# Causal mask of the prompt attention: an addition on VectorE in place of a mask product on TensorE

## What is computed

```python
def fox_attend(q, k, v, cq, ck, q_pos, k_pos):
    s = jnp.einsum('bqhd,bkhd->bhqk', q, k) * (1.0 / math.sqrt(HEAD_DIM))
    decay = jnp.transpose(cq, (0, 2, 1))[..., :, None] - jnp.transpose(ck, (0, 2, 1))[..., None, :]
    mask = k_pos[None, :] <= q_pos[:, None]
    s = jnp.where(mask[None, None], s + decay, -jnp.inf)
    p = jax.nn.softmax(s, axis=-1)
    return jnp.einsum('bhqk,bkhd->bqhd', p.astype(v.dtype), v)
```

## Time and profile before

| what | value |
|---|---|
| median of three runs | 2351.63 us |
| the profiled execution | 2349.69 us |
| its span, first to last instruction | 2347.9 us |
| mean granted TensorE clock | 0.994 |
| PE busy over the span | 2284.9 us (97%) |
| DVE, ACT, POOL busy | 1033.8, 581.4, 632.4 us |

### The profile page before, as it was taken

One profiled execution on the slowest core, in us unless ns is written; L12 is line 12 of the kernel. 1 busy time (PEld: TensorE's weight loads), 2 busy tenths in 40 slices (PEclk: granted clock), 3 DMA queues, 4 the chain that ended last, 5 costly groups with the idle time before them and its releaser, 6 DMA issues. The chain is left out here.

```text
span 2347.9 us, 36305 instructions
## 1 busy us (share of the span) xinstructions
PE 2284.9 (97%) x14220; PEld 2093.6 (89%) x14220; DVE 1033.8 (44%) x1728; ACT 581.4 (25%) x1270; POOL 632.4 (27%) x444
## 2 busy tenths in 40 slices
PE   7999999999999999999989999999999999999998
PEld 7999999999999967777756666799999999999997
DVE  6743332433433756442146777434433323333331
ACT  6420110110100433332135666322110100101101
POOL 6622222232332512100000110453222323222221
PEclk9999999999999999999999999999999999999999
DMA  4111111111111214444464554111111111111111
GB/s 140 40 46 54 46 46 46 46 46 46 46 46 46 90 54 150 134 147 143 155 182 96 126 114 100 36 46 46 45 46 46 46 46 46 46 46 51 48 46 75
DMA packets 194328, 169.96 MB, mean 72 GB/s; under 512 B 28608, under 2 KB 168944, under 8 KB 194167
## 3 DMA queue, kind: packets, MB, share of 16 engines
q1 hardware_dynamic: 153225, 137.71, 20.4%
q10 hardware_dynamic: 40950, 30.02, 4.0%
HBM read 137.55 MB, written 30.50 MB: 72 GB/s over the span
## 5 line engine op out<-in xcount | busy, mean ns | idle before, releaser
L341 PE MATMUL ps<-xn_hi,w_lo 128*128 128x352 f32 x1536 | 497.1, 324 | 5.0 <-DVE h L564 3.2
L494 PE MATMUL ps<-hid_hi,w_lo 128*128 128x352 f32 x1536 | 495.4, 323 | 0.0
L494 PE MATMUL ps<-hid_lo,w_hi 128*128 128x352 f32 x1536 | 492.7, 321 | 0.0
L341 PE MATMUL ps<-xn_lo,w_hi 128*128 128x352 f32 x1536 | 492.4, 321 | 0.0
L341 PE MATMUL ps<-xn_hi,w_hi 128*128 128x352 f32 x1536 | 492.3, 320 | 0.0
L494 PE MATMUL ps<-hid_hi,w_hi 128*128 128x352 f32 x1536 | 492.2, 320 | 0.0
L318 POOL CAST w_hi<-w_raw 128x1024 fp32r<-128x1024 f32 x136 | 142.8, 1050 | 1008.0 <-issue 529.0
L564 DVE TENSOR_TENSOR h<-ps,h 128x352 f32<-128x352 f32 x384 | 198.5, 522 | 446.3 <-PE ps L494 446.3
L532 ACT ACTIVATE tmp_b<-tmp_a 128x352 f32<-128x352 f32 x192 | 95.1, 499 | 1090.6 <-DVE tmp_a L550 1090.6
L320 POOL TENSOR_TENSOR w_lo<-w_raw,w_hi 128x1024 fp32r<-128x1024 f32 x136 | 328.4, 2415 | 10.9
L341 PEld LDWEIGHTS ps<-xn_hi,w_lo 128*128 128x128 f32 x1536 | 288.1, 188 | 7.3 <-DVE h L564 4.3
(11 more groups left out here) (228 smaller groups left out, 2577.4 us busy)
## 6 DMA issues: line engine op xcount, KB each, us to landing
w_raw<-in_w_up SPq DMA_DIRECT2D x64, 512.0 KB, 4.0
w_raw<-in_w_down SPq DMA_DIRECT2D x64, 512.0 KB, 3.4
out<-tok_out ACTq DMA_DIRECT2D x32, 256.0 KB, 2.1
qk_dram<-turn_hi ACTq DMA_DIRECT2D x32, 256.0 KB, 2.4
qk_dram<-turn_lo ACTq DMA_DIRECT2D x32, 256.0 KB, 2.9
k_page<-in_cache_k SPq DMA_DIRECT2D x32, 256.0 KB, 3.3
v_page<-in_cache_v SPq DMA_DIRECT2D x16, 512.0 KB, 9.2
q_a<-qk_dram SPq DMA_DIRECT2D x32, 256.0 KB
```

Of the source, the lines that this page charges most:

```text
L341: last = pe.matmul(ps[:, bank, 0:CH], w, x(k, c), start=(k == 0 and i == 0), stop=(k == nk - 1 and i == 2))
L494: last = pe.matmul(ps[:, NC * (dm % 2) + c, 0:CH], w, x, start=(k == 0 and i == 0), stop=(k == GT - 1 and i == 2))
```

## The change

The mask product leaves score(n); the last product of q_b and k_b now increments q_full. In top(n) DVE first adds an fp32 triangle from SBUF to the diagonal piece in PSUM, in place, waits for that with a semaphore of its own, q_cut, and then takes the maximum over the whole block as before. ident_b and causal_b, both bf16, go from SBUF, and an fp32 tile named causal comes. POOL makes it with a memset and the same selection; its cast of the identity goes. PE no longer waits for the constants, and DVE waits for both steps at block 0.

```diff
@@ prompt_pe, score(n)
-                    pe.matmul(ps[:, b + s // 512, 0:c], q_b[e][0:HD + 2, i * P:w], k_b[e][0:HD + 2, s:s + c],
-                              start=False, stop=(s + c < w))
-                at_ = i * P % 512
-                pe.matmul(ps[:, b + i * P // 512, at_:at_ + P], ident_b[:, :], causal_b[:, :], start=False,
-                          stop=True).then_inc(q_full, 1)
+                    last = pe.matmul(ps[:, b + s // 512, 0:c], q_b[e][0:HD + 2, i * P:w], k_b[e][0:HD + 2, s:s + c],
+                              start=False, stop=True)
+                last.then_inc(q_full, 1)
@@ prompt_dve, top(n)
                 dve.wait_ge(q_full, n + 1)
+                if n == 0:
+                    dve.wait_ge(a_const, 2)
+                diag = scores_of(i)[:, i * P:(i + 1) * P]
+                dve.tensor_tensor(diag, diag, causal[:, :], ALU.add).then_inc(q_cut, 1)
+                dve.wait_ge(q_cut, n + 1)
                 dve.tensor_reduce(stat[:, 0, n % 4:n % 4 + 1], scores_of(i), AX, ALU.max, negate=True).then_inc(q_max, 1)
@@ prompt_const
-            pool.tensor_copy(ident_b[:, :], ident[:, :]).then_inc(a_const, 1)
-            pool.memset(causal_b[:, :], 0.0).then_inc(a_const, 1)
-            pool.wait_ge(a_const, 2)
-            pool.affine_select(out=causal_b[:, :], in_=causal_b[:, :], compare_op=ALU.is_ge, fill=-BIG, base=0,
+            pool.memset(causal[:, :], 0.0).then_inc(a_const, 1)
+            pool.wait_ge(a_const, 1)
+            pool.affine_select(out=causal[:, :], in_=causal[:, :], compare_op=ALU.is_ge, fill=-BIG, base=0,
@@ the stream of PE
-            pe.wait_ge(a_const, 3)
             prompt_pe(pe)
```

More of the change, by code:

```diff
@@ L208, in decoder_step @@
         v_h = [at(f"v_h{i}", [P, NQ, HD], F32, o_tok_at + i * NQ * HD * 4) for i in range(2)]
-        ident_b = att("ident_b", [P, P], BF16)
-        causal_b = att("causal_b", [P, P], BF16)
+        causal = att("causal", [P, P])
         stat = att("stat", [P, 3, 4])
@@ L954, in pe @@
                 pe.drain().then_inc(w_used, 1)
-        o_cut = sem("o_cut")
+        o_cut, q_cut = sem("o_cut"), sem("q_cut")
         proj_o = ProjO()
```

## The result

The changed kernel takes 2372.38 us (median of six runs, 2369.54 to 2375.93) where the kernel before takes 2351.43 (six runs, 2350.84 to 2353.38): a ratio of 1.0088, 95% interval 1.0075 to 1.0101. It is 21 us slower. The prediction had the sign and 2364.4, so +13, and its range ended at 2372.0: the size was wrong. Its profiled execution, the slowest of the six, took 2375.93, 26.2 more than that of before, at a mean granted TensorE clock of 0.981, where the profiled execution of before has 0.994. The other five of the changed kernel have 0.983 to 0.987.

What follows compares the result with a forecast made beforehand. PE was taken to bound one part of each attention head, DVE and ACT the other. 14 x 0.71 = 9.9, plus 0.5, 1.0, 1.0 and 0.4, made 12.8; 2349.69 + 12.8 + 1.94 = 2364.4 us, range 2353 to 2372.

Steps and rivals of the forecast that it cites:

- The two parts of a head: Attention head: PE bounds from block 3's mask product to block 7's; DVE and ACT bound from there to the next block 3's.
- The relief of 0.07 us: PE's score stage: each dropped mask product lets the next weight load start 0.07 us earlier; four count per head, -0.28 us.
- (b): Rival: PE gains nothing from the dropped product, as the width must change anyway; 4 us more, 2368; chance 0.08.
- (c): Rival: each dropped product relieves PE by 0.16 us, 0.35 us a head, 2359 us in all; chance 0.17.
- (f): Rival: PE bounds the whole head and every addition is hidden; faster, 2342.6 us, or 2331 with 0.16; chance 0.09.
- (e): Rival: one paid addition a head, the rest absorbed by shifts in the order; 2355 us (2347 to 2356); chance 0.12.
- The price of 0.33: DVE ahead of each maximum: one addition costs 0.29 us plus 0.04 for its wait, 0.33 us.
- Three additions a head: Three of eight DVE additions are paid (blocks 6, 7, 1; disturbed by POOL: 6, 0, 1): 3 x 0.33 - 4 x 0.07 = +0.71 us.
- at the full granted clock: Attention stage, 283 us: the table of stretches before the change showed PE at the full granted clock.
- E3: Start of block 3's mask product in a head; from there to block 7's (E7) PE bounds, to shorten by 0.28 us.
- Rival (d): DVE bounds everything and all eight additions are paid: 2.36 us a head, 2388 us; chance 0.07.
- The ends: Outside the 15 steps between last blocks: first head +1.0 and +1.0 us, behind the final block 7 +0.4 us.

Runs made afterwards that it cites:

- experiment 6: Kernel after, but only blocks 3, 4 and 5 of each head get DVE's addition; the other five keep PE's mask product: 2346.19 us, ratio 0.9971 to the kernel before.
- experiment 7: Kernel after, but only blocks 0, 1, 6 and 7 get DVE's addition; 2 to 5 keep PE's mask product: 2365.72 us, ratio 1.0059 to the kernel before.
- experiment 1: Kernel before without its mask product and with no addition on DVE, so the causal mask is left out: 2348.97 us, ratio 0.9983.
- experiment 8: Kernel before plus an unused DVE addition into an SBUF scrap tile, which the maximum doesn't wait for: 2363.54 us, ratio 1.0045.
- experiment 2: Kernel after with PE's mask product kept too, so the mask is added twice: 2368.20 us, ratio 1.0066 to the kernel before.
- experiment 4: Kernel after with 6 or 2 unread filler products on PE ahead of block 6's transposes, from the fourth head on: 2362.51 us, ratio 1.0042 to the kernel before.
- experiment 10: Kernel before with DVE additions replacing mask products for blocks 3 to 5 only, and POOL's subtraction in four pieces: 2337.60 us, ratio 0.9940.

## Why the prediction was right and wrong, by its own steps

**The two parts of a head** were right. Experiment 6 moves three additions into the part that PE bounds and they cost nothing; experiment 7 has the four of the other part and shows the whole cost.

**The relief of 0.07 us**, chosen against 0 and 0.16, was right in the rows (the load 0.07 ahead of the modelled end) and in the head (0.3 in experiment 1, against 4 x 0.07). That rules out rivals (b) and (c), and, with 2349 instead of 2342.6 or 2331, (f)'s claim that PE bounds the whole head. Experiment 7 rules out (e), which had one paid addition.

**The price of 0.33** was right: 297 ns plus the wait, 0.34. The disagreement with the Trainium skill's page VectorE: DVE Perf Modes, section The DRAIN you can't avoid, is decided by experiment 8 against 2: the semaphore costs 0.13 us, 0.34 instead of 0.21. The page measured it on eight copies in a row; for an addition with a maximum behind it, it doesn't hold here.

**Three additions a head**, +0.71: right. 17.29 - 16.57 = 0.72 and 18.63 - 17.89 = 0.74 in experiment 4. The disturbed head too comes out as walked: the held normalisation still ends with POOL (2.31 us from a later start), and the heads fit the additions of blocks 6, 0 and 1 being paid.

**The step that failed** is the first one: "at the full granted clock". I read it off the kernel before and carried it into the walk as given. The walk's own steps lengthen the hole of a disturbed head: PE comes to it earlier by six reliefs (E3 to E7 and block 0's, 0.42 us), and the held normalisation ends 0.05 later, 0.47 together; the rows have 1.95 against 1.46. It didn't ask what that does to the clock. The same steps give the hole of each experiment to within 0.03 us, and the traces count the falls:

| kernel | hole before block 6's transposes, us | disturbed heads with a fall |
|---|---|---|
| before, and experiment 6 | 1.46 to 1.48 | 0 of 7 |
| experiment 1 | 1.62 | 1 of 7 |
| experiment 8 | 1.66 to 1.69 | 3 of 7 |
| experiment 2 | 1.80 to 1.81 | 3 of 7 |
| experiment 7 | 1.95 | 5 of 7 |
| after | 1.95 | 6 of 7 |

So the longer hole goes with more falls, and it doesn't fix each of them. Nor does it fix their cost: in experiments 2, 7 and 8 a fall is about half as long as the 6.8 us of the kernel after and costs up to some 0.4 us (0.7 in experiment 1's one), the last head of 2 and 7 aside. What makes the falls of the kernel after long isn't shown; experiment 7, with the same hole and the products of blocks 2 to 5 kept, has short ones.

In the profiled execution six disturbed heads take 1.6 us more than at full clock (20.26 to 20.30, against 18.60 to 18.65 in experiment 4), 10 us. With this term taken out, by fillers, the kernel takes 10.25 us more than before (2362.51 - 2352.26), where my sum has 12.8; with it 21. In the profiled executions the 15 steps alone are 9.35 more (276.08 against 266.73), where I had 10.4. The ends fit less well than the total: 5.1 more up to the first block 7, 2.1 less behind the last. No rival had the clock. Rival (d), the only one above the range, put the excess into DVE, and DVE isn't the bound: it still idles 0.48 us before block 6.

**The ends** were too small by 4 us in the profiled execution: 4.7 instead of 2.0 up to the first block 7, and 1.9 instead of 0.4 behind the last. Not all of the first comes from the additions: 1.5 us are there before the first of them (it starts at 1211.09, the first maximum before at 1209.58), and experiment 1, which has none, gets to its first block 7 2.7 us later than the profiled execution of before. The clock at the start of the stage differs between executions: in 1210 to 1220 it is 1.00 before, 0.83 in experiment 1 and 0.69 after. But experiment 10, with 1.00 in that stretch, also comes 2.6 us later. Behind the last block 7 the clock is 0.71 in 1510 to 1520. How much of the ends is the clock's doing and how much the additions' isn't shown.

```profile
1210.00:1220.00 10.00, 7.55 (x32) 6.26 (x31) 8.14 (x27) 4.34 (x14) 0.00 (x0) 0.69 1.07 365
1510.00:1520.00 10.00, 7.48 (x40) 4.64 (x40) 3.10 (x7) 4.14 (x8) 0.00 (x0) 0.71 0.00 0
```

## What to carry to other kernels

An operation that is moved to an engine with idle time on average is free only where it stands ahead of a wait: read the idle time before each of its places, not the busy share, and move only those (here three of eight, which turned +0.9% into -0.3%). When a change makes a hole on PE longer, price the clock as well, even if it never fell before: look for the longest hole of the old profile and ask what it becomes. The price is a range from nothing up, since the same hole had a fall behind it in some heads and none in others. Two cheap experiments tell this cost from the others: fillers in the hole, and whatever makes the hole taken in smaller pieces.

## What the runs showed of the hardware

- The granted clock went to its lower level behind a hole of 1.95 us in 6 of 7 heads of the kernel after and in 5 of 7 of experiment 7, and in none behind one of 1.46 to 1.48 at the same place. In the kernel after such a fall lasted 6.8 us and cost 1.6; shorter ones, in other kernels, cost 0 to 0.7. In one execution after the other the time of the changed kernel follows the mean clock: 2369.54 us at 0.987, 2372.05 at 0.984, 2375.93 at 0.981.
- More work on PE made the kernel faster: fillers (2362.5 us against 2372.4), and by a little 128 mask products put back (2368.2).
- An addition of 128 columns on DVE takes 297 ns with its output in PSUM, in place. Waiting for it costs 0.13 us over not waiting.
- POOL's subtraction of 1024 columns held DVE's normalisation for 2.65 us; in four pieces it takes POOL 3.61 instead of 2.35 us, DVE gets its turn between them, and that alone is worth 11 us of this kernel (2352.16 - 2340.77).
